# A hybrid decoder step on one core: the index block's cached sample scores issued in pairs into two PSUM banks

## The reference, cut to what matters

```python
def index_scores(qi, ki, wi):
    dots = jnp.einsum('bthd,bsd->bths', qi.astype(F32), ki.astype(F32))
    return jnp.einsum('bth,bths->bts', wi.astype(F32), jax.nn.relu(dots))
```

## Time and profile before

| what | value |
|---|---|
| time, median of 3 runs | 3933.7 us (3931.85 to 3939.8) |
| the profiled execution's own time | 3936.22 us |
| its span, first to last instruction | 3934.4 us |
| PE busy | 3673.2 us (93% of the span) |
| DVE busy | 2112.7 us (54%) |
| ACT busy | 1044.1 us (27%) |
| POOL busy | 1177.4 us (30%) |
| mean granted TensorE clock | 0.943 |

### The profile page before, as it was taken

One profiled execution on the slowest core, in us unless ns is written; L12 is line 12 of the kernel. 1 busy time (PEld: TensorE's weight loads), 2 busy tenths in 40 slices (PEclk: granted clock), 3 DMA queues, 4 the chain that ended last, 5 costly groups with the idle time before them and its releaser, 6 DMA issues. The chain is left out here.

```text
span 3934.4 us, 50715 instructions
## 1 busy us (share of the span) xinstructions
PE 3673.2 (93%) x19290; PEld 2737.8 (70%) x19290; DVE 2112.7 (54%) x4222; ACT 1044.1 (27%) x2164; POOL 1177.4 (30%) x1043
## 2 busy tenths in 40 slices
PE   7999978899898999999989999878999999999998
PEld 4454664467678999999855546644666689999997
DVE  5999565553255333333569995555532553333335
ACT  3301223451232111111442012334412321112123
POOL 3014672313033222222430256723120322222224
PEclk9999956999999999999999999569999999999999
DMA  4111002561212111111121010035512121111111
GB/s 156 49 41 49 6 1 97 180 205 54 75 43 86 43 43 43 43 43 43 35 79 43 31 46 6 1 130 184 168 54 75 43 86 43 43 43 43 43 43 57
DMA packets 145506, 255.08 MB, mean 65 GB/s; under 512 B 25009, under 2 KB 78642, under 8 KB 145074
## 3 DMA queue, kind: packets, MB, share of 16 engines
q1 hardware_dynamic: 132368, 214.92, 16.1%
q0 software_dynamic: 12288, 37.76, 2.7%
q10 hardware_dynamic: 674, 0.09, 0.0%
HBM read 231.31 MB, written 21.42 MB: 64 GB/s over the span
## 5 line engine op out<-in xcount | busy, mean ns | idle before, releaser
L2633 PE MATMUL ps<-ffn_parts 128*128 128x384 f32 (+1 forms) x4608 | 776.7, 329 | 13.2 <-POOL ffn_parts L2823 13.0
L2633 PEld LDWEIGHTS ps<-ffn_parts 128*128 128x128 f32 x4608 | 772.9, 189 | 16.0 <-POOL ffn_parts L2823 13.8
L2643 PE MATMUL ps<-ffn_parts 128*128 128x512 f32 x3328 | 767.9, 390 | 1.9 <-DVE ffn_parts L2888 1.9
L2643 PEld LDWEIGHTS ps<-ffn_parts 128*128 128x128 f32 x3328 | 621.0, 188 | 140.4 <-DVE arena L2901 11.2
L2901 DVE TENSOR_TENSOR arena<-arena,ps 128x1024 f32<-128x1024 f32 x266 | 324.7, 1221 | 299.4 <-PE ps L2643 295.6
L930 PE MATMUL ps<-arena,arena_w 128*128 128x384 f32 (+1 forms) x1152 | 360.4, 476 | 3.6 <-PEq L458 2.6
L939 PE MATMUL ps<-arena_w,arena 128*128 128x512 f32 (+3 forms) x864 | 318.6, 526 | 2.4 <-ACT mix_rest L1115 2.4
L930 PEld LDWEIGHTS ps<-arena,arena_w 128*128 128x128 f32 x1152 | 222.4, 194 | 141.5 <-issue 11.9
L2828 POOL TENSOR_TENSOR ffn_parts<-arena,ffn_parts 128x1024 fp32r<-128x1024 f32 x64 | 154.7, 2419 | 548.0 <-ACT ffn_parts L2719 548.0
L333 DVE TENSOR_SCALAR_CACHE_REDUCE mix_rest<-mix_rest,small 128x384 bf16<-128x384 f32 (+4 forms) x330 | 278.7, 875 | 2.1
L2881 DVE TENSOR_TENSOR arena<-arena 128x384 f32<-128x384 f32 (+1 forms) x96 | 79.5, 854 | 350.3 <-ACT arena L2723 350.3
(11 more groups left out here) (334 smaller groups left out, 5176.5 us busy)
## 6 DMA issues: line engine op xcount, KB each, us to landing
arena<-in_w_down SPq DMA_DIRECT2D x32, 1024.0 KB, 8.6
arena_w<-in_w_in SPq DMA_DIRECT2D x10, 2048.0 KB, 8.2
arena_w<-in_kv SPq DMA_DIRECT2D x64, 256.0 KB
mix_rest<-in_kv SPq DMA_DIRECT2D x64, 256.0 KB
arena<-in_w_up SPq DMA_DIRECT2D x16, 1024.0 KB, 6.8
ffn_raw<-in_w_up SPq DMA_DIRECT2D x14, 1024.0 KB, 6.8
arena<-out_y_prompt SPq DMA_DIRECT2D x2, 4096.0 KB, 14.4
arena_w<-in_mem_kT SPq DMA_DIRECT2D x16, 512.0 KB, 7.3
```

The source lines that it names most:

```text
L2633: ins = pe.matmul(bank(3 * c + b, y - x), w[:, k, :], h[:, k, x:y], start=(k == 0 and h is HH and w is WH), stop=(k == KC - 1 and w is WL))
L2643: ins = pe.matmul(bank((6, 0)[j % 2] + a), u[:, c, tcol(t)] if t < NT - 1 else u[:, c, :], d[:, c, 512 * a:512 * a + 512], start=(first an ...
```

## The change

The 16 units no longer stand one behind each step. They stand in pairs behind every second step: units 0 and 1 behind step 5, 2 and 3 behind step 7, and so on to units 14 and 15 behind step 19. The two units of a pair have the same piece of keys and group of sequences, and differ in `rr_`: the upper and the lower 64 rows. Their two score matmuls are issued one after the other with no wait between them, into bank 7 and bank 5. Bank 5 is also the bank of the turns, so a turn now waits for the relu of every unit scored so far (`s_zr`), and a pair waits until the last turned tile is copied out (`s_qk`). Ahead of a pair PE issues the sums of both units of the pair before. The last two sums stand at the end. ACT reads bank 7 or bank 5 by `rr_`; its order is otherwise by the same list, so both relus of a pair stand behind the relu of the pair's step. ACT's loop over `units_last`, which was empty, is gone.

```diff
-    units_behind, u = {n: [] for n in range(len(steps))}, 0
-    for n in range(5, len(steps)):
-        units_behind[n] = [u]
-        u += 1
-    units_last = list(range(u, len(UNITS)))
+    units_behind = {n: [] for n in range(len(steps))}
+    for p in range(len(UNITS) // 2):
+        units_behind[5 + 2 * p] = [2 * p, 2 * p + 1]
...
+            turned = scored = 0
+
             def turn(j):
+                nonlocal turned
+                turned = j + 1
...
+                if scored:
+                    pe.wait_ge(s_zr, scored)
...
-                else:
+                elif rr_ == 0:
                     pe.wait_ge(s_zr, u)
                 part = slice(64 * rr_, 64 * rr_ + 64)
-                pe.matmul(bank(7), QB[part, g, :], kitc[part, g, 512 * a:512 * a + 512],
+                pe.matmul(bank((7, 5)[rr_]), QB[part, g, :], kitc[part, g, 512 * a:512 * a + 512],
                           start=True, stop=True).then_inc(s_zs, 1)
...
             def sample(u):
+                nonlocal scored
+                if u % 2:
+                    return
                 if u:
+                    sample_sum(u - 2)
                     sample_sum(u - 1)
+                pe.wait_ge(s_qk, turned)
                 sample_score(u)
+                sample_score(u + 1)
+                scored = u + 2
...
-            for u in units_last:
-                sample(u)
+            sample_sum(len(UNITS) - 2)
             sample_sum(len(UNITS) - 1)
...
-                act.activation(rs[:, u // 2 % 2, 512 * rr_:512 * rr_ + 512], bank(7), ACT.Relu).then_inc(s_zr, 1)
+                act.activation(rs[:, u // 2 % 2, 512 * rr_:512 * rr_ + 512], bank((7, 5)[rr_]), ACT.Relu
+                               ).then_inc(s_zr, 1)
```

## The result

| | median | runs |
|---|---|---|
| kernel before | 3935.39 us | 10 runs, 3931.85 to 3941.88 |
| changed kernel | 3950.15 us | 10 runs, 3942.28 to 3959.76 |
| ratio | 1.0037 | 95% interval 1.0026 to 1.0048 |

The change makes the kernel 14.8 us slower (forecast: 13.3). The profiled execution of the changed kernel has a span of 3954.4 us, 20.0 more than the one of before. From the start of step 5 to the mixer's first matmul it takes 68.43 us in layer 0 and 60.65 in layer 1, where before took 55.74 and 55.73.

A forecast was written before the change was run, and what follows sets the result against it. PE was taken to bound the stretch, busy 53.64 of 55.23 us. The PE-ACT loop, +9.7 us over both layers, and clock falls, +3.4, summed to +13.1: 3947 us for the median, range 3940 to 3960.

The forecast's parts named there:

- The pair: Two score matmuls in different rows overlap: 1.05 us, or 2.10 if nothing overlaps; saves 8.4 us of PE per layer.
- the four strips: A step's scores, four heads in four row strips, last 1.14 us where one unit's two passes last 1.12.
- The loop: Step 5 to DVE's end, through PE and ACT every two steps: +4.83 us in layer 0, +9.7 both layers.
- The reading of the loop: On ACT the even step's relu queues behind two unit relus, behind pair and two sums; PE waits for its banks.
- The clock: One more fall to 1.2 GHz per layer, between none and four, at 1.69 us each: +3.4 us.
- The rival with many falls: In the loop, four clock falls a layer at 1.69 us each: 3957 us; chance 0.13.
- DVE did not become the bound: Rival: PE's saving shows until DVE limits, at most 5.4 us per layer faster: 3923 us; chance 0.04.
- the pair does overlap: Rival that pairs do not overlap: each costs 2.10 us, 8.4 us more per layer, 3960 us; chance 0.10.
- something did happen: Rival that little happens: early gain and shorter waits leave under 3.9 us per layer, about 3939 us; chance 0.11.
- One sign missed: Sign to look for in the changed kernel: the block ends some 5 to 8 us later.
- The mixer's start: First matmuls already run at 0.50 clock; no change counted, longer idle could cost or spare about 1.5 us.
- The drains: Tiling-mode changes drain PE, six before and three after per two steps; one spared change credited, at 0.12 us.

The follow-up runs named there:

- units in one strip: Changed kernel with the two units of each pair in the same 64 rows of the array: 3957.23 us against 3933.58, ratio 1.0073.
- gaps filled: Changed kernel with extra matmuls, result not used, on PE behind the scores of steps 6, 10, 14, 16 and 18: 3944.91 us against 3933.58, ratio 1.0027.
- ACT's order alone: Changed kernel with, on ACT only, a pair's two relus behind the following even step's relu: 3943.75 us against 3933.58, ratio 1.0022.
- The sums behind the even step: Changed kernel with the two sums of a pair moved behind the scores of the following even step: 3930.76 us against 3933.58, ratio 0.9991.
- both profiles: The changed kernel, unaltered, profiled twice: spans 3954.4 and 3948.1 us; measured again at 3950.94 us against 3934.12, ratio 1.0046.
- with the block's end filled: Changed kernel with sums moved behind the even step's scores and four extra matmuls behind the last sums: 3927.65 us against 3934.12, ratio 0.9982.
- tails filled: Extra matmuls behind the last sums: changed kernel with extra matmuls in its gaps 3939.19 us, with sums moved 3927.65, kernel before 3932.28, each against 3934.12.

## Why the prediction was right

The direction and the mechanism came out: PE waits once per loop for the even step's relu, and falls of the clock come on top. The size came out too (slower by 14.8 us, forecast 13.3, 3950 inside 3940 to 3960), but that it came so near is in part luck, since one term was too dear and another too cheap. Point by point, in terms of one layer:

- **The pair.** 1.06 us against the 1.05 taken from the four strips, and the end of 2.10 that was kept for the range is what the same rows would cost (1.91). Shown by the trace and by the units in one strip.
- **The loop.** Forecast +4.83 us, measured +3.26 at full clock (gaps filled). By stretches of that kernel: step 5 to the last projection 9.17 us, 1.94 less than before (forecast 1.25); steps 9 to 13 12.68, 0.55 more (1.01); 13 to 19 21.49, 2.99 more (3.47); from 19 on 1.66 more (1.60). All but the last were taken too dear. The scores that wait for a second half were priced right (1.44 for 1.45, 1.67 for 1.67 in the fill), except those of 256 columns at step 7, 1.25 for 1.45. Behind step 9 the two unit relus were too dear, after which ACT goes on 0.97 us from the first one's start (92.85 to 93.82 in layer 0) in place of 1.14, and `summed` behind them, 0.47 (to 94.29) in place of 0.57; behind step 13 they take 1.11 and 0.61.
- **The reading of the loop.** That the even step's relu is late because it stands behind the unit relus was the smaller part of it. ACT's order alone takes 0.05 to 0.58 us off a gap, 1.9 of 6.9 us per layer. What matters is that nothing stands on PE between the scores of an even step and those of the next odd one. The sums behind the even step show it from the other side: ACT's order as changed, gaps gone.
- **The clock.** This is the term that was mis-sized: one fall of 1.69 us per layer forecast, three of 3.1 and one of 1.65 in both profiles, 11.1 us in place of 3.4. The three of layer 0 last long enough to slow scores, sums and pair, where I priced one by a projection of 16 matmuls. The loop was 3.2 us too dear (9.7 for 6.5), the falls by the profiles 7.7 us too cheap; a fall fewer ahead of step 5 and the mixer's start took 2.8 us off again in the first profile. By the medians filling the gaps is worth less, 1.0037 and 1.0046 against 1.0027, 4 to 7 us; the 6.8 us that are left of the 11.1 when the fill's slower mixer start is counted agree with that.
- **The rival with many falls** (3957) had the right picture of layer 0, while its number would have been 7 us too high. The others fell: DVE did not become the bound until the sums were moved, the pair does overlap, and something did happen. One sign missed: the block should end 5 to 8 us later, and it ended 12.69 later in layer 0 (three falls) and 4.92 in layer 1 (one).
- **The mixer's start.** I counted no change and left 1.5 us either way. In the first profile it was +0.12 and -1.42. With the gaps filled it was +1.5 twice. Ahead of all of these PE had idled 3.35 us, so the idle's length does not tell which of them comes.
- **The drains** of which the Trainium skill (TensorEngine Tiling (Array Packing), Key Properties) speaks: two sums in a row take 1.86 us where two apart take 2.00, and two units in one strip 1.91 where two apart take 2.10. That is 0.14 to 0.19 us for each spared change of shape, in agreement with the rule and near the 0.12 that the sum held. No run sets a drain apart from what else a lone instruction costs, and none shows what the further spared changes gave.

## What to carry to other kernels

When work that is packed tighter is also moved, look at what it covered where it stood: here 2 us of PE work between two steps hid a relu's way through ACT and back, and the saved 1.05 us per pair was less than the uncovered wait. Packing pays when the freed order still leaves something between a producer and the next use of its banks; moving two sums was enough to turn +14.8 us into about -3 (its interval reaches no change), and into -6.5 with the block's end filled. And where short gaps lower TensorE's clock, as four of these did, a gap costs more than its length, so that even extra work in the gap can make a kernel faster.

## What the runs showed of the hardware that was not expected

- Extra matmuls gave time back: with the gaps filled the two blocks together took 11.1 us less (117.99 against 129.08), because no stretch fell to 1.2 GHz.
- Behind 1.32 us of idle the mixer ran at 1.2 GHz for some 3 us (before), behind 3.77 and 3.78 for 5 us (sums moved), behind 0.47 to 0.59 (tails filled) not at all. Behind 3.35 us it did all three: some 3 us in layer 0 of the changed kernel, 6 us with the gaps filled, and in layer 1 of the changed kernel, in both its profiles, it started at full clock.
- Two units in different rows start together and cost what one does, to 0.01 us (1.06 against 1.05).
